# Widening the MLP up projections' matmuls to both parts of the input, with the two half sums added on evacuation

## The reference, cut to what matters

```python
SEQ, D_MODEL, D_FF = 256, 1024, 4096

def sq_relu_mlp(h, w1, w2):          # h: 256 x 1024, w1: 1024 x 4096, w2: 4096 x 1024
    a = jax.nn.relu(h @ w1)
    return (a * a) @ w2

for i in range(2):
    ...
    h = h + rms_norm(mix, norm_g[i, 1])
    ff = sq_relu_mlp(rms_norm(h, norm_g[i, 2]), mlp_w1[i], mlp_w2[i])
    h = h + rms_norm(ff, norm_g[i, 3])
```

## Time and profile before

| | |
|---|---|
| median of 3 runs | 1434.42 us |
| time of the profiled execution | 1436.3 us |
| its span in the profile | 1434.3 us |
| mean granted TensorE clock | 0.93 of full |
| busy: TensorE matmul, weight load | 91%, 81% of the span |
| busy: VectorE, ScalarE, GpSimd | 64%, 47%, 36% |
| DMA | 197.12 MB, mean 137 GB/s |

### The profile page before, as it was taken

How to read it: one execution, slowest core, us unless ns; L and a number is a source line. 1 busy time by engine, 2 the same in 40 slices (tenths; PEclk the granted TensorE clock), 3 DMA queues, 4 the chain that set the end, 5 groups by cost and what they waited for, 6 DMA issues and landing times.

```text
span 1434.3 us, 21569 instructions
## 1 busy us (share of the span) xinstructions
PE 1309.8 (91%) x7997; PEld 1156.9 (81%) x8002; DVE 916.2 (64%) x1382; ACT 668.9 (47%) x1128; POOL 514.2 (36%) x260
## 2 busy tenths in 40 slices
PE   5876999998889899999899999898989967899998
PEld 5775999997656699998788888797888855799998
DVE  6767433336755533333673776488999887499997
ACT  5634444444335544444454544344444542356553
POOL 3103544444600444444334321142332321345543
PEclk9557999998958899999799999999999987999999
DMA  7012666554200566665366432353443421455663
GB/s 242 0 59 88 208 192 186 177 170 133 86 29 29 167 214 178 184 191 156 103 192 190 147 101 77 88 148 118 133 131 117 139 95 57 110 180 183 192 191 115
DMA packets 170428, 197.12 MB, mean 137 GB/s; under 512 B 14077, under 2 KB 135421, under 8 KB 170365
## 3 DMA queue, kind: packets, MB, share of 16 engines
q1 hardware_dynamic: 169147, 192.07, 43.9%
q10 hardware_dynamic: 1218, 4.21, 0.8%
HBM read 195.20 MB, written 1.05 MB: 137 GB/s over the span
## 4 chain that ended last, share of the span: by engine, by line
PE 71%; DVE 20%; ACT 3%; issue 3%; DMA 1%; POOL 1%; DVEq 0%; SPq 0%; ACTq 0%
PE acc L623 22%; PE wk L578 12%; PE wk L579 11%; PE wk L580 11%; DVE LO L446 2%; DVE arena L2313 2%; PE wk L879 2%; DVE arena L2261 1%; DVE arena L2297 1%; PE acc L578 1%; DVE arena L2325 1%; PE wk L1000 1%; PE acc L1026 1%; PE wk L689 1%; PE acc L579 1%
## 5 line engine op out<-in xcount | busy, mean ns | idle before, releaser
L446 POOL TENSOR_TENSOR LO<-raw,HI 128x1024 fp32r<-128x1024 f32 (+3 forms) x191 | 463.5, 2432 | 819.5 <-ACT HI L1240 819.3
L1240 ACT ACTIVATE HI<-raw 128x1024 fp32r<-128x1024 f32 (+3 forms) x382 | 364.3, 996 | 151.4 <-PE acc L623 71.0
L578 PE MATMUL wk<-XH,HI 128*128 128x256 f32 x1296 | 376.5, 291 | 29.7 <-DVE XL L1964 11.8
L579 PE MATMUL wk<-XL,HI 128*128 128x256 f32 x1296 | 372.7, 288 | 0.0
L580 PE MATMUL wk<-XH,LO 128*128 128x256 f32 x1296 | 372.2, 287 | 0.0
L446 DVE TENSOR_TENSOR LO<-raw,HI 128x1024 fp32r<-128x1024 f32 (+3 forms) x191 | 241.0, 1264 | 176.0 <-ACT HI L1240 175.7
L578 PEld LDWEIGHTS wk<-XH,HI 128*128 128x128 f32 x1296 | 254.7, 197 | 37.4 <-issue 14.9
L579 PEld LDWEIGHTS wk<-XL,HI 128*128 128x128 f32 x1296 | 254.9, 197 | 2.0
L580 PEld LDWEIGHTS wk<-XH,LO 128*128 128x128 f32 x1296 | 254.6, 196 | 0.0
L623 PE MATMUL acc<-HI,HH 128*128 128x512 f32 x424 | 133.1, 395 | 13.7 <-DVE HL L2304 13.0
L623 PE MATMUL acc<-LO,HH 128*128 128x512 f32 x424 | 132.0, 393 | 0.0
(11 more groups left out here) (346 smaller groups left out, 1929.4 us busy)
## 6 DMA issues: line engine op xcount, KB each, us to landing
raw<-in_mlp_w SPq DMA_DIRECT2D x128, 512.0 KB, 4.1
raw<-in_w_in SPq DMA_DIRECT2D x100, 512.0 KB, 4.0
raw<-in_w_up SPq DMA_DIRECT2D x44, 512.0 KB, 3.9
raw<-in_w_down SPq DMA_DIRECT2D x44, 256.0 KB, 3.2
raw<-in_att_w_in SPq DMA_DIRECT2D x16, 512.0 KB, 4.3
raw<-in_w_ssd_proj SPq DMA_DIRECT2D x16, 512.0 KB, 3.6
raw<-in_att_w_out SPq DMA_DIRECT2D x8, 512.0 KB, 4.2
raw<-in_w_out SPq DMA_DIRECT2D x8, 512.0 KB, 3.4
```

The costliest lines, as they stand in the source:

```text
L446: tensor_tensor(LO[:, s, cs], raw[:, s % 2, "ab".index(part), 0:m], HI[:, s, cs].bitcast(F32), ALU.subtract).then_inc(S(f"lo_{part}"), 1)
L578: mm(o, lh, rh, start=start, stop=False, skip_group_check=skip)
L579: mm(o, lh, rl, start=False, stop=False, skip_group_check=skip)
L1240: A(HI[:, s, j * m:(j + 1) * m], raw[:, s % 2, j, 0:m], ACT.Copy).then_inc(S(f"hi_{part}"), 1)
```

## The change

`XH` and `XL` become two planes of one tensor `XX`, so that for a tile k the 256 columns of the high part and the 256 of the low part stand side by side. In the MLP up projections one matmul of 512 columns multiplies the weight tile's high part with both; it fills a whole PSUM bank. A second matmul of 256 columns adds the product of the weight tile's low part and the input's high part to the first half of that bank. A chunk now takes two banks, one for each j, and the two chunks in flight take all four. The halves of each bank are added on evacuation: ScalarE copies the second halves to `relu_b`, VectorE adds the first halves, then makes max(x, 0)·x with one instruction into `sq_b`; ScalarE copies that to `HH`, and VectorE subtracts as before. ScalarE's second step, `hidden_high`, stands behind the next conversion of a ring piece. All other users of `XH` and `XL` see the same views with another stride.

In the diff, the first `hidden` is ScalarE's and the last one VectorE's.

```diff
-        XH = sb("XH", [P, KD, SEQ], F32R)
-        XL = sb("XL", [P, KD, SEQ], F32R)
+        XX = sb("XX", [P, KD, 2, SEQ], F32R)
+        XH, XL = XX[:, :, 0, :], XX[:, :, 1, :]
...
+            def ch_major_wide(s, par, norm=None):
+
+                for j in range(2):
+                    for k in range(KD):
+                        w = k * 256 + j * P
+                        if norm is not None and j == 0:
+                            xT_wait(norm, 1, k)
+                        mm(wk[:, 2 * par + j, :], HI[:, s, w:w + P], XX[:, k, :, :], start=(k == 0), stop=False,
+                           skip_group_check=True)
+                        last = mm(wk[:, 2 * par + j, 0:SEQ], LO[:, s, w:w + P], XH[:, k, :], start=False,
+                                  stop=(k == KD - 1), skip_group_check=True)
+                return last
...
-                    used(ch_major(s, par, norm=1 + 2 * layer if isinstance(c, int) and c == 0 else None))
+                    used(ch_major_wide(s, par, norm=1 + 2 * layer if isinstance(c, int) and c == 0 else None))
...
                 def hidden(c, par, piece):
 
                     done(piece)
-                    if not (isinstance(c, int) and c + base < 2):
-                        act.wait_ge(S("hid_lo"), c + base - 1)
-                    A(relu_b[:, par, :], wk[:, par, :], ACT.Relu).then_inc(S("hid_read"), 1)
-                    act.wait_ge(S("hid_read"), c + base + 1)
-                    A(HH[:, par, :, :], relu_b[:, par, :].rearrange("p (j t) -> p j t", j=2), ACT.Square)\
+                    A(relu_b[:, par, :].rearrange("p (j t) -> p j t", j=2), wk[:, 2 * par:2 * par + 2, SEQ:2 * SEQ], ACT.Copy)\
+                        .then_inc(S("hid_part"), 1)
+
+                def hidden_high(c, par):
+
+                    act.wait_ge(S("hid_squared"), c + base + 1)
+                    A(HH[:, par, :, :], sq_b[:, par, :].rearrange("p (j t) -> p j t", j=2), ACT.Copy)\
                         .then_inc(S("hid_hi"), 1)
 
                 hi_to(first + 3)
                 hidden(0, 0, first)
+                hidden_high(0, 0)
 
                 def turn(c, piece):
                     hi_next()
                     hidden(c + 1, 1, piece)
                     hi_next()
+                    hidden_high(c + 1, 1)
                     hi_next()
                     hidden(c + 2, 0, piece + 2)
                     hi_next()
+                    hidden_high(c + 2, 0)
...
                 hidden(MC - 1, 1, first + 2 * MC - 3)
+                hidden_high(MC - 1, 1)
...
                 def hidden(c, par):
 
+                    dve.wait_ge(S("hid_part"), c + base + 1)
+                    part = relu_b[:, par, :].rearrange("p (j t) -> p j t", j=2)
+                    TT(part, wk[:, 2 * par:2 * par + 2, 0:SEQ], part, ALU.add).then_inc(S("hid_read"), 1)
                     dve.wait_ge(S("hid_read"), c + base + 1)
-                    link(TT(sq_b[:, par, :], relu_b[:, par, :], relu_b[:, par, :], ALU.mult))
+                    STT(sq_b[:, par, :], relu_b[:, par, :], 0.0, relu_b[:, par, :], ALU.max, ALU.mult)\
+                        .then_inc(S("hid_squared"), 1)
+                    dve.wait_ge(S("hid_squared"), c + base + 1)
                     dve.wait_ge(S("hid_hi"), c + base + 1)
                     TT(HL[:, par, :, :], sq_b[:, par, :].rearrange("p (j t) -> p j t", j=2),
                        HH[:, par, :, :].bitcast(F32), ALU.subtract).then_inc(S("hid_lo"), 1)
```

More of the change, by code:

```diff
@@ L2025, in mlp @@
                     ring.enter(i, 1)
-                    steps.enter(i, 2)
                     lo_next()
@@ L2033, in mlp @@
                 ring.leave((MC - 2) // 2)
-                steps.leave((MC - 2) // 2)
                 lo_to(first + 2 * MC)
```

## The result

The changed kernel takes 1423.67 us, the median of 7 runs (1422.81 to 1433.06); the kernel before beside it 1434.42 us (7 runs, 1429.64 to 1440.34). The ratio is 0.993, with a 95% interval of 0.9915 to 0.9945: 10.8 us faster, and outside the predicted range on the fast side. Two later sets of the same kernel gave 1425.64 and 1425.06 us beside 1434.86 and 1435.66 of before. The profiled execution took 1425.37 us.

The account below looks back on a forecast made before the run. TensorE's matmul stream was taken to bound both MLPs. Its saving of 6.5 us, with the evacuation at cost 0, took the median from 1434.4 to 1427.9 us; the range was 1425.0 to 1432.5 us.

Parts of the forecast that it names:

- What bounds the kernel: In both MLPs time is TensorE's stream alone; what the change takes off it moves the stage's end equally.
- TensorE's part: MLP up projections: a tile costs 0.3471 us instead of 0.3600; 496 of 512 tiles save, 6.5 us in all.
- rows 4 and 5: Profile spacings in MLP pieces and second block's projection: 512 columns cost 0.0129 us less than two times 256.
- Rival 1: MLP up pieces: the fixed price stays, perhaps through alternating lengths; 1434.4 us with all, 1431.2 with half; chance 0.10.
- rows 7: Profile spacing at the lower clock: 0.2133 us a step, exactly 256 columns at 1.2 GHz, so merging saves nothing there.
- The evacuation: Behind up pieces: longer ScalarE and VectorE chain, subtract ending 4.3 us after the piece, all hidden, cost 0.
- T + 5.5: Behind an up piece ending at T: the next piece but one's two loads issue together 5.5 us later.
- rival 2: Stages behind the MLPs: the gain is given back through other clock steps; 1430 to 1434 us, chance 0.07.
- 2 us either way: Stages behind the MLPs: range allowance for clock steps, from three earlier runs spreading over 3.7 us without any change.
- Rivals 3 and 4: Weight ring feeds TensorE late, 1439 us or more, chance 0.03; short matmul's 0.013 us also saved, 1421.5 us, chance 0.04.

Follow-up runs that it names:

- with the matmuls apart: Changed kernel with each half chunk's eight 512-column matmuls first, then its eight of 256 columns, instead of in turns: 1427.4 us, ratio 0.9947.
- the changed kernel covered: Changed kernel with 20 matmuls of zeros ahead of the transposes of each of the last six norms: 1427.51 us, ratio 0.9941.

## Why the prediction was right or wrong

**What bounds the kernel**: right. After the change the waits of TensorE in the MLP are one of 0.7 us at its start, none for `LO` or `HL`.

**TensorE's part**: the mechanism was right, the term mis-sized. The fixed price was found where rows 4 and 5 put it, and with the matmuls apart an up piece costs 5.56 us, as forecast. The step that failed is that it takes "a stream of alternating 512 and 256 columns to cost the sum of both", which the text itself had marked as shown by no row: it cost 0.3525 us a pair instead of 0.3471, and the saving was 3.8 to 4.0 us instead of 6.5. Rival 1 named the place, the alternation, at "half of the price", 1431.2, and that was its size; its chance of 0.10 was too low for something no row showed. At the half clock nothing is saved, as rows 7 had it: in the first up piece of the changed kernel's second profile, four pairs from 145.59 to 148.15 us take 0.64 each, three times 0.2133. The Trainium skill's 2.5 ns a matmul ("TensorE: Matmul & The Clock Gate", section "Wait — 56ns, not 53.3ns?") would have given 1.2 us, the prediction's estimate from that page. The measured 4.0 lies between it and the 6.5 of the rows' 13 ns, and with the matmuls apart the trace shows the 13 ns in full.

**The evacuation**: cost 0 was right, shown by the kernel with the new evacuation and the old matmuls (ratio 1.0007). One duration was wrong: the subtract ends 5.7 us behind the up piece (201.39 to 207.11), not 4.3, since it takes 2.40 us beside GpSimd. The Trainium skill says it, in "SBUF — State Buffer", section "🔬 SBUF: two separate sides": a VectorE operation with two SBUF inputs and a GpSimd operation that reads SBUF exclude each other for a whole instruction. The trace agrees in the main: GpSimd's operation ends at 206.55 and the subtract, begun at 204.71, at 207.11, 0.56 us later, where it takes 0.69 alone. The prediction had the two side by side and put 0.69. The low part behind the subtract ends later too, and the two loads behind it are issued at 208.40, T + 7.0 and not T + 5.5; the cover of 11 us made all of that harmless.

**The range and rival 2**: here the prediction failed. Its step "Their time holds steps of granted clock that fall where they fall", with "2 us either way" for them, took the clock as scatter from run to run, and rival 2 expected it to give gain back, not to add to it. It is not mainly scatter. The share of the attention stage at the half clock follows from where the stage begins against the clock's changes, and shortening the MLP by 2 us usually moves the kernel from a dear place (163.1 us) to a cheap one (157.5): 5.5 us. With the direct 4.0 that makes 9.5 of the 10.8; the last 1.3 lie in small differences of the other stages, the SSD branch's 1.0 above all, and no run takes them apart. That this place was the cheap one is luck: 5 more useless matmuls, 1.1 us, lose most of it. The direct term was 2.5 us too large and the other 6.8 us were missing, so the forecast came within 4.2 us of the result partly because two errors of opposite sign met.

**Rivals 3 and 4**: neither came. The weight ring kept up, with landings of 4.7 us in the median of all MLP loads, where the page of before has 4.1.

**Left open.** Why one long and one short matmul in turns cost 0.0055 us more, and why not in every piece. Why a kernel meets another place in some runs: the changed kernel's third profile, an execution of 1431.46 us, has 164.7 us where the first two have 157.6 and 157.5, and three more of its 21 runs lie at 1433.1 to 1435.6. Why the places at 3.9 and 6.1 us have two values each. The theory gives the usual value and its sign, not each run.

## What to carry to other kernels

Merging two matmuls of 256 columns into one of 512 saves the fixed price of one weight load and matmul, about 0.013 us here, and only at the full clock; two of one length together cost less than one and one in turns, which gave two fifths of it back (5.57 us for a piece and not 5.64; the whole kernel was slower for it all the same, by its place). In a kernel with stages at both levels of the clock, an edit of a few microseconds can, as here, move the stages behind it against the changes of the clock and win or lose more than its own worth: compare stage by stage at equal granted clock, and try the same edit with a microsecond or two of useless work beside it before crediting or blaming the edit. Here seven matmuls of zeros bought half of what the change did.

## What the runs showed of the hardware that I had not expected

Useless work of 1.6 us made the kernel before 5.2 us faster (1431.03 beside 1436.23), and 3.2 us of it didn't. One 512- and one 256-column matmul in turns take 0.353 us in all pieces read but the first, two and two 0.348 a pair, eight and eight 0.3475. A VectorE subtract of 128 x 512 took 2.40 us beside a GpSimd operation and 0.69 us without one. The attention stage took 157.4 to 164.8 us for the same matmuls, by where it met the clock's changes. A higher mean clock was not a shorter time: 0.944 and a span of 1427.1 us for the changed kernel covered, 0.936 and 1423.4 uncovered, since some of the covering work held TensorE up.
